# A hybrid decoder layer on one core: second query buffer, later embedding transposes, re-timed maximum, split exponentials, fused key products

## What is computed

```python
h = layer_norm(x)
rq, rk, rv, rg, fq, fk, fv, ff, gr, gf = split(h @ w_in)
o_r, state = retention(rope(rq), rope(rk), rv)      # prompt in chunks; sample from a recurrent state
o_f = forgetting_attention(fq, fk, fv, log_sigmoid(ff + b_f))   # sample: over 1024 past tokens in pages
mix = (sigmoid(gr) * (norm_gate(o_r, rg) @ w_ret_proj) + sigmoid(gf) * (o_f @ w_fox_proj)) @ w_out
x1 = layer_norm(ALPHA * h + mix)
ffn = (silu(x1 @ w1) * (x1 @ w3)) @ w2
ple = sigmoid(x1 @ w_pg) * (p @ w_pe)               # p: per-layer embedding
y = layer_norm(ALPHA * x1 + ffn + ple)
```

## Time and profile before

| | us |
|---|---|
| median of 3 runs | 1841.12 |
| lowest, highest | 1840.11, 1842.10 |
| the profiled execution | 1845.44 |
| its span, first to last instruction | 1843.9 |
| TensorE busy in it | 1759.3 |
| VectorE, ScalarE busy | 1068.4, 772.0 |
| mean granted TensorE clock | 0.98 |

### The profile page before, as it was taken

One profiled execution on the slowest core, in us unless ns is written; L12 is line 12 of the kernel. 1 busy time (PEld: TensorE's weight loads), 2 busy tenths in 40 slices (PEclk: granted clock), 3 DMA queues, 4 the chain that ended last, 5 costly groups with the idle time before them and its releaser, 6 DMA issues.

```text
span 1843.9 us, 37985 instructions
## 1 busy us (share of the span) xinstructions
PE 1759.3 (95%) x14751; PEld 1706.7 (93%) x14751; DVE 1068.4 (58%) x1203; ACT 772.0 (42%) x906; POOL 145.7 (8%) x236
## 2 busy tenths in 40 slices
PE   6999889989899999999879999999999999999996
PEld 5999789889899899999879999999999999999995
DVE  6467576766767644576564555554444555544554
ACT  4443423423433343443354455554333444443333
POOL 5001111111011110000000000000000000000000
PEclk9999999989899999999989999999999999999998
DMA  6758578678599987555435577775555777765551
GB/s 198 220 176 275 195 254 306 203 245 297 183 314 335 344 283 224 168 183 183 131 117 185 178 238 239 237 242 181 178 180 184 220 238 233 242 190 175 177 164 47
DMA packets 316559, 394.71 MB, mean 214 GB/s; under 512 B 12720, under 2 KB 289456, under 8 KB 316072
## 3 DMA queue, kind: packets, MB, share of 16 engines
q1 hardware_dynamic: 286832, 287.48, 49.7%
q0 software_dynamic: 29280, 105.79, 16.6%
q10 hardware_dynamic: 352, 0.12, 0.0%
HBM read 379.50 MB, written 13.84 MB: 213 GB/s over the span
## 4 chain that ended last, share of the span: by engine, by line
PE 84%; DVE 7%; DMA 4%; ACT 2%; issue 1%; POOL 0%; POOLq 0%; SPq 0%; ACTq 0%; DVEq 0%
PE acc L553 26%; PE acc L558 25%; PE acc L554 25%; DMA page<-in_cache_v 2%; DVE wlo L484 1%; DMA qbc<-q_rows 1%; PE X L655 1%; PE X L887 1%; DVE page L1343 1%; DVE sc L1344 1%; ACT whi L479 1%; DMA raw<-in_w_in 1%; DVE uT L1652 0%; PE X L772 0%; DVE sqR L1459 0%
## 5 line engine op out<-in xcount | busy, mean ns | idle before, releaser
L484 DVE TENSOR_TENSOR wlo<-raw,whi 128x1024 fp32r<-128x1024 f32 (+1 forms) x552 | 660.5, 1204 | 610.7 <-ACT whi L479 602.3
L479 ACT ACTIVATE whi<-raw 128x1024 fp32r<-128x1024 f32 (+1 forms) x552 | 569.3, 1037 | 670.9 <-PE acc L558 638.9
L553 PE MATMUL acc<-x_hi,whi 128*128 128x264 f32 x1664 | 412.6, 285 | 10.4 <-DVE x_lo L1661 6.8
L554 PE MATMUL acc<-x_lo,whi 128*128 128x264 f32 x1664 | 410.8, 284 | 0.0
L553 PE MATMUL acc<-hT_hi,whi 128*128 128x264 f32 x1408 | 370.5, 299 | 8.2 <-DVE scd L1327 5.8
L554 PE MATMUL acc<-hT_lo,whi 128*128 128x264 f32 x1408 | 357.4, 289 | 0.0
L553 PEld LDWEIGHTS acc<-x_hi,whi 128*128 128x128 f32 x1664 | 314.0, 189 | 11.4 <-issue 7.2
L554 PEld LDWEIGHTS acc<-x_lo,whi 128*128 128x128 f32 x1664 | 314.3, 189 | 0.0
L553 PEld LDWEIGHTS acc<-hT_hi,whi 128*128 128x128 f32 x1408 | 273.4, 194 | 24.7 <-issue 15.0
L554 PEld LDWEIGHTS acc<-hT_lo,whi 128*128 128x128 f32 x1408 | 273.8, 194 | 0.5 <-issue 0.2
L558 PE MATMUL acc<-x_hi,wlo 128*128 128x264 f32 x1664 | 236.9, 286 | 0.0
(11 more groups left out here) (333 smaller groups left out, 1574.3 us busy)
## 6 DMA issues: line engine op xcount, KB each, us to landing
raw<-in_w SPq DMA_DIRECT2D x256, 512.0 KB, 4.2
raw<-in_w_in SPq DMA_DIRECT2D x176, 512.0 KB, 5.5
page<-in_cache_k POOLq DMA_DIRECT2D x64, 512.0 KB, 5.7
page<-in_cache_v POOLq DMA_DIRECT2D x64, 512.0 KB, 5.3
raw<-in_w_out SPq DMA_DIRECT2D x32, 512.0 KB, 4.5
raw<-in_w_pg SPq DMA_DIRECT2D x32, 512.0 KB, 3.5
stateS<-in_state_ret POOLq DMA_DIRECT2D x8, 1024.0 KB, 8.9
raw<-in_w_fox_proj SPq DMA_DIRECT2D x16, 512.0 KB, 3.8
```

The lines of the kernel that those rows point to most:

```text
L479: nc.scalar.activation(slot_of(whi, s)[:, 0:k, :], raw[:, s, 0:k, :], ACT.Copy).then_inc(S["hi_made"], 1)
L484: nc.vector.tensor_tensor(slot_of(wlo, s)[:, 0:k, :], raw[:, s, 0:k, :], slot_of(whi, s)[:, 0:k, :].bitcast(F32), ALU.subtract).then_inc(S ...
L553: mm(backward(acc[c.acc][:, m, 0:T]), w, backward(xh[:, c.kt0 + t, :]), start=c.first and t == 0, stop=False)
L554: mm(backward(acc[c.acc][:, m, 0:T]), w, backward(xl[:, c.kt0 + t, :]), start=False, stop=False)
```

## The change

- FIRST is 20 instead of 21, and the turn starts at the first chunk of a group: 40, 56, 72, 88, 108, 124, 140, 156. Keys are used one chunk earlier. The spread (L677) comes two chunks behind the transposed maximum instead of one, subtraction three instead of two, exponentials four instead of three, pp five instead of four. So spread and subtraction stay at the chunks at which they were, and values move by at most one chunk.
- The query has two buffers and two semaphores. The first two requests' rows are loaded at once; those of request b from the third on at the first key of request b - 1, when request b - 2's keys are used. The second buffer lies where the embedding's transposed parts go later.
- Each key page is handled by eight `tensor_tensor_reduce`, one for each head, instead of one product and one reduction; the program has two instructions for each, the product and a read of the accumulator.
- The prompt's exponentials are done for two heads at j = 9 and for two at j = 10, with the whi of a chunk between them; normalising moves from j = 10 to j = 11.
- The embedding is transposed behind chunk 190 instead of 5, into other banks of X; its two loads move on GpSimd's queue from the start to behind the last state load, and its copy and subtraction ahead of phYR. TensorE waits for them ahead of phP.
- The queries' rows are transposed and stored one chunk earlier (j = 0 of phF).

The diff, cut to its core:

```diff
-FIRST, STEP = 21, 17
+FIRST, STEP = 20, 17
...
-    return (1 - window(b)) % 4
+    return -window(b) % 4
...
-        return 5 + p
-    first = turn(b) + 5
+        return 6 + p
+    first = turn(b) + 6
...
+        qbc = [qbc, place("qbc1", [P, 1024], F32, at=made["pT_hi"][0])]
...
-        ptok = place("ptok", [P, 3, 256], F32, at=after("wff"))
-        prow = place("prow", [104, P], F32, at=after("ptok"))
+        ptok = place("ptok", [P, 3, 256], F32, at=made["page"][0])
+        prow = place("prow", [104, P], F32, at=after("wff"))
...
-                    if pos == 1:
+                    if pos == 2:
                         other, done = idle_acc(ph, it, j)
...
-                    if pos == 2:
+                    if pos == 3:
                         pe.wait_ge(S["sx_made"], b + 1)
...
-                    if it == 0 and j == 1:
+                    if it == 0 and j == 0:
                         query_rows()
...
+                if j == 14:
+                    entry_T()
                 if j == 12:
...
-                    if g == window(b) + turn(b) + 3:
+                    if g == window(b) + turn(b) + 4:
                         act.wait_ge(S["sx_made"], b + 1)
...
-                    if j == 9:
+                    if j in (9, 10):
                         act.wait_ge(S["f_score_sb"], it + 1)
-                        for i in range(4):
+                        for i in range(j * 2 - 18, j * 2 - 16):
                             A(prob4[:, i, 0:P], prob4[:, i, 0:P], ACT.Exp, bias=softs[:, i:i + 1], accum_out=softs[:, 8 + i:9 + i])
...
-                    if pos == 2:
+                    if pos == 3:
                         dve.wait_ge(S["pmaxS_ps"], b + 1)
...
-                    if pos == 4:
+                    if pos == 5:
                         dve.wait_ge(S["exp_made"], b + 1)
...
-                        dve.wait_ge(S["q_in"], b * 16 + 16)
+                        dve.wait_ge(q_in[b % 2], b // 2 * 16 + 16)
...
-                    link.step(V.tensor_tensor(page[:, s, :], page[:, s, :], qbc[:, :], ALU.mult))
-                    V.tensor_reduce(sc8[:, p, :], page[:, s, :].rearrange("s (h d) -> s h d", h=H_F), axis=AX.X, op=ALU.add)\
-                        .then_inc(S["page_used"], 1)
+                    for i in range(H_F):
+                        head = page[:, s, i * P:(i + 1) * P]
+                        last = V.tensor_tensor_reduce(out=head, in0=head, in1=qbc[b % 2][:, i * P:(i + 1) * P], scale=1.0, scalar=0.0,
+                                                      op0=ALU.mult, op1=ALU.add, accum_out=sc8[:, p, i:i + 1])
+                    last.then_inc(S["page_used"], 1)
...
-                    if j == 10:
-                        dve.wait_ge(S["f_exp"], it + 1)
+                    if j == 11:
+                        dve.wait_ge(S["f_exp"], it * 2 + 2)
                         link.step(V.reciprocal(softs[:, 8:16], softs[:, 8:16]))
...
-            pool.dma_start(bf[:, :], a["b_f"].rearrange("(o n) -> o n", o=1).partition_broadcast(P)).then_inc(S["bf_in"], 16)
-            pool.dma_start(ptok[:, 0:2, :], a["p_prompt"].rearrange("(t p) d -> p t d", p=P)).then_inc(S["p_in"], 16)
-            pool.dma_start(ptok[0:DEC, 2, :], a["p_sample"]).then_inc(S["p_in"], 16)
+            pool.dma_start(bf[:, :], a["b_f"].rearrange("(o n) -> o n", o=1).partition_broadcast(P)).then_inc(S["wff_in"], 16)
...
-                pool.wait_ge(S["page_used"], NPG * b + 1)
-                pool.dma_start(qbc[:, :], q_rows[b:b + 1, :].partition_broadcast(P)).then_inc(S["q_in"], 16)
+                if b >= 2:
+                    pool.wait_ge(S["page_used"], NPG * (b - 1) + 1)
+                pool.dma_start(qbc[b % 2][:, :], q_rows[b:b + 1, :].partition_broadcast(P)).then_inc(q_in[b % 2], 16)
...
+            load_query(1)
...
-                for b in range(1, DEC):
-                    if due(FIRST + STEP * (b - 1) + KEY_POS[-1] + 1):
+                for b in range(2, DEC):
+                    if due(FIRST + STEP * (b - 1) + 1):
                         load_query(b)
...
+            pool.wait_ge(S["pv_ps"], DEC * NPG + 1)
+            pool.dma_start(ptok[:, 0:2, :], a["p_prompt"].rearrange("(t p) d -> p t d", p=P)).then_inc(S["p_in"], 16)
+            pool.dma_start(ptok[0:DEC, 2, :], a["p_sample"]).then_inc(S["p_in"], 16)
```

31 lines of the change are left out of this document (16 added, 15 removed).

## The result

The changed kernel takes **1820.7 us** (median of 4 runs, 1819.41 to 1823.68), the kernel before 1841.61 beside it: a ratio of 0.9889, 95% interval 0.9872 to 0.9906. The forecast was 1827.3 in a range of 1816 to 1845. The direction and the range hold; the gain is 20.9 us where 13.8 were summed up.

The account below looks back on a forecast made before the run. TensorE, 95% busy, was taken as the bound, losing time to decode waits and the lower clock behind them. Terms 6.0 + 2.7 + 1.4 + 2.3 + 2.4 + 3.0 - 3.0 - 1.0 = 13.8 us, 1841.1 to 1827.3; range 1816 to 1845.

Parts of the forecast that it names:

- From below: ... 2.25: Low estimate of a fused key on VectorE: 0.20 plus 0.08 per head, times eight, 2.25 us; 2.4 was taken.
- Each 1 us above costs some 12: Price of a key longer than 2.4 us: some 12 us per 1 us, counted once or twice in about nine places.
- request 3: Chunks 88 to 92: later spread and earlier query gain 6.0 of 11.5 us; 2.55 us wait behind 91 stays.
- request 1: Chunks 58 to 60: the 2.32 us wait goes, 2.55 at chunk 59 stays; gain 2.7 us.
- transposes at 29: Behind chunk 29 TensorE waits 2.1 us for the probabilities instead of 0.3; loss taken as 3.0 us.
- pages 82, 84: The late page wait at 84 is replaced by about 4 us of wait at chunk 82; gain 0.
- request 4: A VectorE chain through reciprocal, key and oR; two waits become one of about 6 us at 111, gain 0.
- page at 152: State load issued some 3.5 us earlier against the page behind it; gain 3.0 us (0 to 4.4).
- The waits only move: Rival, chance 0.17: sx, 82 and 29 take over more waiting than allotted; 6 us less, some 1834.
- Half rate: Rival, chance 0.14: accumulating products run at two cycles per element, key 3.3 us, 11 us more, some 1838 to 1842.
- Full latency: Every fused operation takes its whole length, key 3.65 us; together with half rate 4.0 us.
- VectorE becomes the bound: Rival, chance 0.14, the slower side: from a key of 3.9 us VectorE limits phR; 1851 us at a key of 4.0.

Follow-up runs that it names:

- a_oldkey: Changed kernel with product and reduction (two instructions of 1024) for each key page again, all else as changed: 1828.09 us, ratio 0.9921 to the kernel before.
- a_key41: Changed kernel with two extra reductions of 1024 ahead of each key's fused operations, a key of 4.2 us: 1868.54 us, ratio 1.0141 to the kernel before.
- b_again: The kernel before once more, unchanged, for a second profile: 1841.12 us, ratio 0.9992.
- a_oldkeyturn: Changed kernel with old two-instruction keys and old turn; two query buffers, late embedding and split exponentials stay: 1834.57 us, ratio 0.9964 to the kernel before.
- b_buffers: The kernel before with only two query buffers loaded a request ahead and the later embedding: 1834.04 us, ratio 0.9951.
- a_exp1: Changed kernel with the prompt's exponentials in one part again (all eight at j = 9, normalising at j = 10): 1825.35 us, ratio 0.9913 to the kernel before.
- a_sxfirst: Changed kernel with the spread maximum's subtraction moved on VectorE ahead of its chunk's wlo and rotary steps: 1811.95 us, ratio 0.9829 to the kernel before.
- a_sx2: a_sxfirst with the subtraction of requests 0 and 4 one iteration earlier still: 1810.94 us, ratio 0.9832 to the kernel before.
- best1: a_sx2 with the new token's products moved from behind the retention's last result to chunk 107: 1809.08 us, ratio 0.9822 to the kernel before.

## Why the prediction was right, and where it was off

The working can be checked as it stands by a_oldkey, since the sum took 2.4 us for a key: forecast 1827.3, measured 1828.1. The 7.4 us between that and the changed kernel are one term, **the key**, at 1.70 to 1.76 us instead of 2.4. The step that failed is "From below: ... 2.25": I took the spacing of neighbours without a wait (0.34 for 264 elements) as a length of 0.20 for 128 plus a full 0.08 for the read. The 0.20 was nearly right, but the read begins with the next head's instruction and adds nothing, so that what counts is 0.21 a head. ScalarE's pair, whose read begins 0.09 ahead of the next, had shown an overlap; I used it to choose the low side and then took a value above it. "Each 1 us above costs some 12" fits below 2.4 us (11.4), but above, where it was meant, a_key41 measured 22. One reading of a row was off too, without consequence: VectorE's idle for qbc at request 3 is 4.05 us in the earlier trace rows, not 3.9.

By place, as the length of the same chunks in each trace less that in the first trace of before:

| place (chunks) | forecast | long keys (a_oldkey) | changed |
|---|---|---|---|
| request 3 (88 to 92) | -6.0 | -6.9 | -8.2 |
| request 1 (58 to 61) | -2.7 | -2.3 | -1.5 |
| requests 2 and 5 (74, 75; 124 to 147) | -1.4 | -1.7 | -2.2 |
| request 0 (42 to 45) | -2.3 | -2.9 | -3.6 |
| values 48, 53 (46 to 57) | -2.4 | -0.9 | -2.5 |
| transposes at 29 (28 to 31) | +3.0 | +1.8 | +1.1 |
| pages 82, 84 (76 to 87) | 0 | -0.6 | -3.4 |
| request 4 (108 to 115) | 0 | -1.7 | -3.2 |
| page at 152 (148 to 155) | -3.0 | -3.6 | -3.6 |
| values two chunks behind their key, and 156 (measured: 116 to 123 only) | +1.0 | +1.2 | +0.7 |

Two terms of this table are weaker than they look, since b_again, with nothing changed, has -3.2 for the page at 152 and +2.7 for request 1. Against that trace the changed kernel wins 0.5 and 4.2 there. So the agreement at 152 (3.0 forecast, 3.6 measured) is in part luck of the trace from which the sum was made.

Request 3, the largest term, went as worked out: the new wait for pmax that was forecast at chunk 88 with 1.2 us is there with 0.37, the spread is in time, and the 2.55 us at 91 stay to the hundredth. But the spread a chunk later has no share in it that shows: with the old turn and long keys the place gains 8.2 in a_oldkeyturn and 5.8 in b_buffers. The surplus is mostly clock. The rule that I read from before, that every idle stretch of 2.05 us or more is followed by the lower level, doesn't hold: the clock is 1.00 over chunks 88 to 92 with those 2.55 us in it, where a_oldkey has 0.92 with the same wait, and so has a_exp1 with short keys. At 82 it stayed up after 2.68 as well. The trace of before had already spoken against the rule, behind the 2.32 us at 58:

```profile
257.08:260.50 3.42, 3.42 (x26) 3.24 (x26) 0.95 (x1) 0.00 (x0) 0.00 (x0) 1.00 1.05 379
```

Request 4 was called a closed chain with gain 0. That two waits become one of about 6 us at 111 was right (6.3 with long keys, 5.6 with short ones). But there were three waits on that chain: with one long wait at 111, TensorE comes to the new products at 113 later than they do, and the wait of 2.16 us there, with a fall of the clock, is gone in both kernels (chunks 113 to 115 are 4.0 us shorter in both, 108 to 112 are 2.3 and 0.8 longer). The step "the two waits become one ... with the same end" stopped a chunk or two too early. a_sxfirst, a_sx2 and best1 show the same chain from the other side.

At 82 and 84 the wait moved two chunks as forecast ("about 4 us of wait there instead": 3.94 in a_oldkey, 2.68 here). In the changed kernel it is the key, again, that made it shorter: all six kernels with the short key and the new turn have 2.57 to 2.84 us there.

Request 1 gained less than forecast (1.5 instead of 2.7), which is within what b_again shows for this place. The wait at 59, 3.40 instead of 2.55, has a reason that stood in none of the rivals, as far as the traces show it: the DMA engines are full around chunk 57 (a share of 1.05), and a TensorE that no longer waits for a page there waits for what late weights delay.

**The rivals.** *The waits only move* was wrong for this change, and right for each of the last three kernels here. *Half rate*, an estimate of 0.13 us more for a head from the rows of 1.23 for 1024 elements and 0.289 for 128: 0.21 us for a head excludes it; the 0.28 that one instruction lasts is that of a plain one of 128 elements (0.289). *Full latency*, every operation at its whole length, is excluded by the rows of 128.51 and 128.72: an operation of 0.28 is followed after 0.21. *VectorE becomes the bound* didn't come up. a_key41, with a key of 4.2 us, shows that its point of 3.9 was put too low: VectorE's 239.5 us in chunks 48 to 111 are still less than TensorE's 253.7. And its 1851 for a key of 4.0 was too low, with 1868.5 measured at 4.2. The price is paid in waits at single places, pages above all. Where between 2.4 and 4.2 it rises, three lengths can't tell, and beyond that nothing was run.

**What stays open.** The difference of the traces is 26.0 us, that of the medians 20.9. Both profiled executions of before lie 4 to 5 us above their median, those of the changed kernel and of a_oldkey at or below theirs. So the traces give more than the medians, -17.5 (1845.4 to 1827.9) against -14.2 (1842.3 to 1828.1) for a_oldkey, and the agreement of 1828.1 with 1827.3 has some luck in it: against the trace from which it was made the sum is 4 us short (1831.6 forecast for an execution like the profiled one), by request 4 and chunk 29 above all, and the profiled executions of before had about that much too much. Why the short key wins 11.8 us alone and 7.4 to 8.1 beside the second query buffer was not followed either. Which waits are shorter in an execution without profile can't be seen. What part of the 7.8 us of b_buffers is the embedding's wasn't run alone; by the traces its transposes cost 1.0 at either place.

## What to carry to other kernels

When an operation has no row, look in its neighbours' rows for when the next one begins, not for how long it lasts, and look for the same pair on another engine. Ask for each engine that gets faster what it sets free, and what that then collides with: here the shorter key took most of the page waits away (6.5 us in a_oldkey, 2.7 in the changed kernel), and where the transfers were full (a DMA share of 1.05 around chunk 57) late weights seem to have taken a page's place. And where several small steps end one behind the other at one place, as at chunks 108 to 116, moving one of them names the next; a sum of waits is not a gain until the chain behind them has been followed to its end.
